# Kernel for a hybrid attention, retention and mixture-of-experts layer: the last experts' rows summed in the banks

## The reference: what is computed

```python
# g_sel: best of 4 groups; expert_id: the 2 best of its 8 experts; 32 experts in all
hid = jax.nn.silu(xb @ w_gate[e]) * (xb @ w_up[e])      # 2048 -> 512
y   = (hid @ w_down[e]) * row_w                          # 512 -> 2048
out = segment_sum(y, row_tok)                            # back to the tokens
x   = layer_norm(alpha * x + out, ln2_scale, ln2_bias)
```

## Time and profile before

| what | us |
|---|---|
| runs, median (lowest to highest) | 2056.97 (2056.35 to 2057.52) |
| the profiled execution | 2061.3 |
| its span, first to last instruction | 2059.5 |
| TensorE busy in the span | 1783.2 |
| VectorE, ScalarE busy | 995.0, 751.4 |

### The profile page before, as it was taken

How to read it: one execution, slowest core, us unless ns; L and a number is a source line. 1 busy time by engine, 2 the same in 40 slices (tenths; PEclk the granted TensorE clock), 3 DMA queues, 4 the chain that set the end, 5 groups by cost and what they waited for, 6 DMA issues and landing times.

```text
span 2059.5 us, 25116 instructions
## 1 busy us (share of the span) xinstructions
PE 1783.2 (87%) x9868; PEld 1151.2 (56%) x9868; DVE 995.0 (48%) x1469; ACT 751.4 (36%) x1321; POOL 15.3 (1%) x34
## 2 busy tenths in 40 slices
PE   9999999999999999999999977766776676666677
PEld 7888888888888888888888532211221122112222
DVE  5454454555444444566565555344433443344357
ACT  5444444344444444454453423122222222122221
POOL 0000000000000000000000000000000000000000
PEclk9999999999999999999999978777787777777778
DMA  7556655455556555466677999999999999999998
GB/s 246 193 176 191 197 176 178 148 184 188 190 184 192 171 186 176 154 191 234 221 278 290 378 430 421 429 433 432 431 433 431 432 432 430 433 431 433 431 427 335
DMA packets 131010, 615.07 MB, mean 299 GB/s; under 512 B 13108, under 2 KB 13780, under 8 KB 116720
## 3 DMA queue, kind: packets, MB, share of 16 engines
q1 hardware_dynamic: 130208, 611.74, 77.0%
q0 software_dynamic: 720, 2.18, 0.6%
HBM read 609.61 MB, written 2.36 MB: 297 GB/s over the span
## 4 chain that ended last, share of the span: by engine, by line
PE 60%; DMA 26%; issue 10%; DVE 2%; ACT 1%; DVEq 0%; POOL 0%; POOLq 0%; SPq 0%; ACTq 0%
DMA W<-in_w_expert_up_dram 25%; PE PS L603 14%; PE PS L605 14%; PE PS L604 14%; PE PS L1217 11%; PE PS L1194 2%; PE PS L1150 1%; PE PS L983 1%; PE PS L1259 1%; DVE ZACC L2267 1%; PE PS L1330 0%; DMA VC<-VS 0%; PE PS L1073 0%; PE PS L960 0%; DMA XN<-in_x_dram 0%
## 5 line engine op out<-in xcount | busy, mean ns | idle before, releaser
L580 DVE TENSOR_TENSOR WL<-RAW,WH 128x1024 fp32r<-128x1024 f32 x384 | 457.5, 1222 | 400.4 <-ACT WH L576 399.1
L576 ACT ACTIVATE WH<-RAW 128x1024 fp32r<-128x1024 f32 x384 | 394.6, 1058 | 260.8 <-PE PS L605 198.9
L603 PE MATMUL PS<-WH,XH 128*128 128x512 f32 x1216 | 479.9, 395 | 0.1
L605 PE MATMUL PS<-WH,XL 128*128 128x512 f32 x1216 | 474.0, 390 | 0.0
L604 PE MATMUL PS<-WL,XH 128*128 128x512 f32 x1216 | 473.2, 389 | 0.0
L1217 PE MATMUL PS<-W,XE 128*32 128x512 f32 x1728 | 244.8, 730 | 120.2 <-DMA W<-in_w_expert_up_dram 120.2
L603 PEld LDWEIGHTS PS<-WH,XH 128*128 128x128 f32 x1216 | 228.3, 188 | 49.5 <-issue 1.7
L605 PEld LDWEIGHTS PS<-WH,XL 128*128 128x128 f32 x1216 | 228.2, 188 | 48.6
L604 PEld LDWEIGHTS PS<-WL,XH 128*128 128x128 f32 x1216 | 228.5, 188 | 45.4
L1217 PEld LDWEIGHTS PS<-W,XE 128*32 128x32 f32 x1728 | 62.4, 131 | 321.9 <-issue 210.3
L2218 DVE TENSOR_TENSOR GSUM_H<-PS,GB 32x512 f32<-32x512 f32 x31 | 21.0, 678 | 363.0 <-ACT UB L1671 363.0
(11 more groups left out here) (335 smaller groups left out, 1530.8 us busy)
## 6 DMA issues: line engine op xcount, KB each, us to landing
RAW<-in_w_in_dram SPq DMA_DIRECT2D x304, 512.0 KB, 4.5
W<-in_w_expert_down_dram SPq DMA_DIRECT2D x28, 4096.0 KB, 29.0
W<-in_w_expert_gate_dram SPq DMA_DIRECT2D x27, 4096.0 KB, 34.8
W<-in_w_expert_up_dram SPq DMA_DIRECT2D x27, 4096.0 KB, 19.9
RAW<-in_w_branch_ret_dram SPq DMA_DIRECT2D x32, 512.0 KB, 5.1
RAW<-in_w_out_dram SPq DMA_DIRECT2D x32, 512.0 KB, 5.8
W<-in_w_expert_down_dram SPq DMA_DIRECT2D x7, 2048.0 KB, 28.1
W<-in_w_expert_gate_dram SPq DMA_DIRECT2D x7, 2048.0 KB, 10.9
```

The costliest lines, as they stand in the source:

```text
L576: act.activation(WH[:, i % RING], RAW[:, i % RING], ACT.Copy).then_inc(hi_done, 1)
L580: dve.tensor_tensor(WL[:, i % RING], RAW[:, i % RING], WH[:, i % RING].bitcast(F32), ALU.subtract).then_inc(lo_done, 1)
L603: pe.matmul(PS[:, bank + t], hs, wh, start=first and j == 0, stop=False)
L605: mm = pe.matmul(PS[:, bank + t], ls, wh, start=False, stop=end)
```

## The change

Four things at the end of the expert pipeline:

- On VectorE the weights and tokens of 30 come ahead of `add_rows(28, 0)`, and the gating of 30 and `add_rows(28, 1)` ahead of the tables. On ScalarE the tanh of 30 comes after the first half of `rows_scaled(31)`.
- The down products of 30 go to XE_BANK, from a hidden buffer of its own (HT30), right behind those of 29, whose parts get buffers of their own (YH29, YL29).
- The rows of 29 and 30 are summed in the SPREAD banks (`spread_29`, `spread_30`, `spread_both`), and VectorE adds each bank pair once (`add_both`) instead of twice.
- `spread_norm2` 2 and 3 come ahead of the second half of the last `gate_up`, and on VectorE all of `norm_rows` ahead of `hidden_last`. Two matmuls of `keep_busy` remain there where three were.

```diff
+                    if bank == XE_BANK:
+                        pe.wait_ge(xe_stored, NE * QS)
+                    elif not first:
                         pe.wait_ge(y_dve, item)
...
+        def spread_part(t, m, gs, y, start, stop):
...
+            rows = slice(m * ROWS, (m + 1) * ROWS)
+            return pe.matmul(PS[:, SPREAD + m], gs[rows, t * P:(t + 1) * P], y[rows, :], start=start, stop=stop)
...
+        def spread_29():
...
+            pe.wait_ge(g_ready, NE - 2)
+            pe.wait_ge(added, (NE - 3) * 4 + 2)
+            pe.wait_ge(y_dve, NE - 2)
+            for y in (YH29, YL29):
+                for m in range(QD):
+                    spread_part(0, m, GS29, y, y is YH29, False)
+        def spread_30():
...
+            for m in range(QD):
+                spread_part(0, m, GS30, YH, False, False)
+            pe.wait_ge(y_dve, NE - 1)
+            for m in range(QD):
+                mm = spread_part(0, m, GS30, YL, False, True)
+                if m % 2:
+                    mm.then_inc(spread, 2)
+        def spread_both(n):
+            pe.wait_ge(added, (NE - 3) * 4 + 4 + 2 * n)
+            for gs, y in ((GS29, YH29), (GS29, YL29), (GS30, YH), (GS30, YL)):
+                for m in range(2 * n, 2 * n + 2):
+                    mm = spread_part(1, m, gs, y, y is YH29, y is YL)
+            mm.then_inc(spread, 2)
...
         spread_rows(NE - 4, 1)
+        turn_hidden(NE - 2)
         down(NE - 3, 1, (2, 3), halves=True)
-        pe.wait_ge(h_ready, NE - 1)
-        turn_hidden(NE - 2)
-        spread_rows(NE - 3, 0, GS29, by_pairs=True)
-        down(NE - 2, 2, (0, 1), halves=True)
-        spread_rows(NE - 3, 1, GS29, by_pairs=True)
-        down(NE - 2, 2, (2, 3), halves=True)
-        pe.wait_ge(xe_stored, NE * QS)
-        keep_busy(XE_BANK, 1, rid, Z[:, 0, 0:CH])
-        for t in range(TOK):
-            spread_rows(NE - 2, t, GS30, by_pairs=True)
-            if t == 0:
-                keep_busy(XE_BANK, 2, rid, Z[:, 0, 0:CH])
+        down(NE - 2, 2, range(KH), halves=True, ht=HT30, bank=XE_BANK)
+        spread_29()
+        keep_busy(GU_BANK, 1, rid, Z[:, 0, 0:CH])
+        spread_30()
+        keep_busy(GU_BANK, 1, rid, Z[:, 0, 0:CH])
+        for n in range(2):
+            spread_both(n)
         number_slots()
         spread_compact(0)
-        spread_norm2(0)
+        for j in range(2):
+            spread_norm2(j)
         gate_up(NE - 1, 3, 0, take(1), last=True)
-        spread_norm2(1)
         spread_compact(1)
         gather_sums()
+        for j in range(2, 4):
+            spread_norm2(j)
         gate_up(NE - 1, 3, 1, take(1), last=True)
-        spread_norm2(3)
...
+        rows_scaled(NE - 1, 1, range(1))
         hidden_tanh(NE - 2)
-        rows_scaled(NE - 1, 1)
-        y_high(NE - 3, W29)
-        hidden_copy(NE - 2)
-        y_high(NE - 2, W30)
+        rows_scaled(NE - 1, 1, range(1, QS))
+        hidden_copy(NE - 2, HT30)
...
+        hidden(NE - 2)
+        add_rows(NE - 4, 1)
         for t in range(TOK):
             last = dve.tensor_scalar(TOKV[:, t:t + 1], RC[:, R_P:R_P + 1], float(QD),
...
-        hidden(NE - 2)
-        add_rows(NE - 4, 1)
-        y_low(NE - 3, W29)
+        y_low(NE - 3, W29, high=YH29, low=YL29)
+        y_low(NE - 2, W30, bank=XE_BANK)
         for t in range(TOK):
-            add_rows(NE - 3, t)
-        y_low(NE - 2, W30)
-        for t in range(TOK):
-            add_rows(NE - 2, t)
+            add_both(t)
         row_stats()
...
-        for j in range(2):
+        for j in range(4):
             norm_rows(j, 0)
-        centre_rows(2, 0)
         hidden_last()
-        scale_rows(2, 0)
-        norm_rows(3, 0)
```

More of the change, by code:

```diff
@@ L469, in build @@
     RSTD3 = at("RSTD3", 198.47, [1])
+    YH29 = at("YH29", 44, [QC], F32R)
+    YL29 = at("YL29", 46, [QC], F32R)
+    HT30 = at("HT30", 30.5, [KH, ROWS])
     OB = at("OB", 112, [TOK, D])
@@ L1238, in turn_hidden_more, with down @@
             mm.then_inc(h_turned, 1)
-        def down(item, k4, blocks, first=False, halves=False, more=False):
+        def down(item, k4, blocks, first=False, halves=False, more=False, ht=HT, bank=Y_BANK):
             pair_q = MORE_PAIRS[2] if more else LAST_PLACES[2, item] if halves else place(2, k4) % PAIRS
@@ L1258, in down @@
                     col = (b % KB2) * D + m * QC
-                    mm = pe.matmul(PS[m * ROWS:(m + 1) * ROWS, Y_BANK], HT[:, b],
+                    mm = pe.matmul(PS[m * ROWS:(m + 1) * ROWS, bank], ht[:, b],
                                    W[pair_q][:, b // KB2, col:col + QC], start=b == 0, stop=b == KH - 1)
@@ L1320, in spread_rows @@
                 pe.wait_ge(y_act, item + 1)
-            if not by_pairs:
-                pe.wait_ge(added, item * 4 + 2 * t + 2)
+            pe.wait_ge(added, item * 4 + 2 * t + 2)
             for part, y in ((0, YH), (1, YL)):
@@ L1326, in spread_rows @@
                 for m in range(QD):
-                    if by_pairs and part == 0 and m % 2 == 0:
-                        pe.wait_ge(added, item * 4 + 2 * t + 1 + m // 2)
                     rows = slice(m * ROWS, (m + 1) * ROWS)
-                    mm = pe.matmul(PS[:, SPREAD + m], gs[rows, t * P:(t + 1) * P], y[rows, :],
+                    mm = pe.matmul(PS[:, SPREAD + m], GS[rows, t * P:(t + 1) * P], y[rows, :],
                                    start=part == 0, stop=part == 1)
@@ L1357, in spread_norm2 @@
                 pe.wait_ge(ln2_low, 1)
-            if j < 2:
-                pe.wait_ge(added, (NE - 1 + run) * 4 + 1 + j)
+            if j < 2 and run:
+                pe.wait_ge(added, NE * 4 + 1 + j)
+            elif j < 2:
+                pe.wait_ge(added, (NE - 1) * 4 + 2 * j)
             if j >= 2:
@@ L1679, in rows_copy, with rows_scaled @@
             act.activation(xg(item)[:], PS[:, xe_bank(item)], ACT.Copy).then_inc(xg_stored, 1)
-        def rows_scaled(item, buf):
+        def rows_scaled(item, buf, parts=range(QS)):
             first = isinstance(item, int) and item < 2
             act.wait_ge(xe_turned, item + 1)
-            for j in range(QS):
+            for j in parts:
                 for k in range(KQ):
@@ L2267, in add_rows, with add_both @@
                 dve.tensor_tensor(z, PS[:, SPREAD + 2 * n:SPREAD + 2 * n + 2], z, ALU.add).then_inc(added, 1)
+        def add_both(t):
+            for n in range(2):
+                dve.wait_ge(spread, (NE - 3) * 4 + 4 * t + 2 * n + 2)
+                z = ZACC[:, t, n * 2 * QC:(n + 1) * 2 * QC].rearrange("p (m c) -> p m c", m=2)
+                dve.tensor_tensor(z, PS[:, SPREAD + 2 * n:SPREAD + 2 * n + 2], z, ALU.add).then_inc(added, 2)
         def row_stats():
```

27 lines of the change are left out of this document (17 added, 10 removed).

## The result

The changed kernel takes 2063.79 us (median of 11 runs, 2061.01 to 2065.91) beside 2058.37 for the one before (11 runs, 2056.35 to 2060.11). The ratio is 1.0027 with an interval of [1.0019, 1.0035]: slower by 5.4 us, and beyond the top of the range of the prediction (2062.0). The three runs that the prediction started from had put the kernel before at 2056.97, 1.4 lower than the eleven do.

What follows compares the result with a forecast made beforehand. Bound: the second store and LZ ending together, LZ hanging on the gating of 31. Between +0.2 (full clock) and +2.4 (half clock) it took +2.0: 2063.3 for the profile, 2059.0 for the median, range 2055.7 to 2062.0.

Steps and rivals of the forecast that it cites:

- Gating of 30: VectorE and ScalarE: HB of 30 ready at 2006.8 instead of 2010.29, 3.5 us earlier.
- Down products of 30: TensorE: wait for weights until 2012.1 and 2017.0, end at 2020.4; of the 3.5 us, 0.4 are left.
- Rows summed in the banks: From the products of 30 to the last add: 7.1 instead of 7.5, four adds back to back.
- TensorE behind the adds: Gate and up of 31 start at 2028.5 to 2029.2 behind the second spread_norm2; last half at 2039.7 to 2040.0.
- The lower clock on the last half: Last 32 gate and up matmuls, nearer the slow row: +2.4 at half clock, +0.2 at full; +2.0 taken.
- A sum of +2.0: Whole kernel: loss in us taken between +0.2 and +2.4, the last gate and up partly at full clock.
- The gating behind all norms: VectorE: gating of 31 not before 2044.4, 0.25 later than before; at the slow price 2046.7, 2.5 later.
- The second store: End of kernel: issued 7 us earlier, lands long before LZ, worth 0.1.
- The end: Last 32 down products of 31: 3.64 in the sum, with no cost for the idleness in front of them.
- a rival, with 0.20: Last 32 down products at the lower clock take 6.4 instead of 3.64: +2.7 more, 2061.7 to 2062.0; chance 0.20.

Runs made afterwards that it cites:

- the repairs: Changed kernel with VectorE's old order at the end and four fills (LAST_FILL = 4) ahead of the turning of 31, together: 2062.77, ratio 1.0015 to the kernel before.

## Why the prediction was wrong

- **Gating of 30: right.** HB was done at 2004.42. In this execution the gate and up products of 30 were 2.27 early, so 2006.8 becomes about 2004.5. Nothing behind it became late.
- **Down products of 30: right.** They waited for their weights twice, the second time until 2016.34, took 3.40 and ended at 2019.74. With the landing 0.7 later that is the 2020.4 I took. The weights set the end of this piece, so the early gating brought no more.
- **Rows summed in the banks: wrong by a little.** The prediction gave 7.1 from the products to the last add, with four adds back to back. It was 7.45. The fill (2020.34, 1.13) holds the rows of 30 up until 2021.39, though YH is there earlier, and 0.23 lies between the adds (2024.83). The 0.4 that I gave to the sums is gone: half the adds, and no gain. VectorE still waits for rows ahead of both adds (0.95 and 0.23). The Trainium skill ("Trainium Kernel Development and Optimization", Best Practices) says only that tiling doesn't speed up the evacuation of the banks; that each add taken away is then saved was my reading, and 7.47 against 7.45 doesn't bear it out.
- **TensorE behind the adds: wrong path.** The prediction had the first spread_norm2 done beside the last add and only the second behind it, so that gate and up "start at 2028.5 to 2029.2", 1.0 to 1.7 behind the adds at 2027.5. The first one began at 2027.07, with the adds nearly done (2027.19), and both stood on the path at the lower clock's price, 1.71 each (4 x 0.43; at 1.00 four took 1.03, from 2039.68 to 2040.71). The half started at 2030.61, 3.42 behind the adds. I had the earlier trace rows say that the half runs at the lower clock, and did not ask what that makes of the matmuls in front of it.
- **The lower clock on the last half: wrong place.** "the last 32 gate and up matmuls in over 5 us with PEclk near 0.5" was the sign that I named, and a 3.8 there was to prove me wrong. The second half took 3.64 at a clock of 1.00, and 3.64 in every profile in which it stands whole. What I took for idleness, a wait for the second block, was not there in the changed kernel: TensorE came so late that VectorE waited 2.49 for it. Where the wait was there, 1.09 in the new order alone, the half behind it took 3.64 too.
- **These two errors cancelled, and that is luck.** A sum of +2.0 with adds 0.8 earlier has the products end near 2045.6, about 18 behind the adds. They ended at 2045.36, 18.17 behind: the last half started at 2041.72, 1.7 to 2.0 late, as the first half before it had, and was some 2 shorter than the sum had it.
- **The gating behind all norms: the mechanism was right, the size was off.** The norms ended at 2046.59, not 2044.4, because they waited for the late spread_norm2. The gating lost 0.49 behind GB (2046.02), where the prediction gave 0.25, and only for products that end early; at +2.0 its sum had the products last and nothing for this.
- **The second store: right in kind.** It was issued at 2046.6, 4.8 earlier than before where I had 7, and had landed when LZ was done.
- **The end: the step that failed.** The sum kept the last 32 down products at 3.64 and put the idleness in front of them at nothing; it stood only as a rival, with 0.20, an idle 1.5 and last products of 6.4. The idle was 2.15 and the products took 5.13 at 0.52 and 0.62, 1.49 more. With the 0.46 that the gating lost more than before (0.49 less 0.03) this is the 1.95 by which the last piece is longer. Filled, that end took 3.64 (LAST_FILL = 4); left empty in the old order it took 5.25, and the runs lost 1.8. The rule of the Trainium skill ("TensorE: Matmul & The Clock Gate", Part 1) that the clock is low unless activity releases it fits the end, with 0.52 behind the idle stretch. It doesn't account for 2026 to 2030, where the profile has TensorE busy 2.00 of 2.00 and the clock at 0.55 and 0.50.

So the sum gave the profile +2.0 and it came to +4.08: -1.12 up to the adds (I had -0.8), +3.00 to the products (about +2.9), +1.95 to LZ (nothing), and 0.25 behind. The median missed by 4.8. Of this 2.1 is what the profile shows, nearly all of it that end, 1.4 is the base of three runs, and 1.3 is that the medians differ by 5.42 and the two profiled executions by 4.08; no run says where that part lies.

Shown by runs: the order behind the adds is the loss (1.0031 alone, 1.0005 without it); an empty end costs 1.8 (1.001 in the old order). Less sure: VectorE's order is a third to a half of the loss (0.0014 between the ratios, 0.0008 with the end filled, intervals that overlap). Read from profiles only: that fills ahead of the first half were paid at the lower clock, and how the loss divides between the two pieces. Open: what lowers the clock where the adds end, why it falls at another point in other executions, and whether the repairs add. A stretch of 4.2 us behind LZ is 5.1 to 5.7 in four of the profiles; there the last write, of LZ, takes 3.6 to 4.1 from issue to landing, and 2.7 in all others. All four have the whole new order on TensorE, but so have the changed kernel and the one with the end filled, which show 2.7; whether the order brings this about is open too, and it may hold a part of the 1.3. No version was clearly faster than the kernel before.

## What to carry to other kernels

Where the profile shows that a stretch of TensorE runs at the lower clock, price every instruction that you add inside it at that clock too. Before an operation that does off-path work is moved ahead of the critical one, ask what it filled where it stood: here the spread_norm2 behind the last products kept TensorE occupied, and without it the idle in front of the turning was 2.15 instead of 0.58. Taking away half of an engine's work gains nothing while it waits for its input: here VectorE still waited for rows ahead of both double adds.

## What the runs showed that I had not expected

- TensorE can be busy without a break and yet be granted 0.50: in 2026 to 2030 after, with 4-row matmuls, and in 2026 to 2034 of the kernel with fills among them, full matmuls included.
- The same idleness, 1.70 us, was followed by 3.64 in one execution, by 5.08 and 5.34 in two others; 0.59 or less was followed by 3.64 in all seven profiles that have it, and 2.15 or more by 4.97 to 5.25 in three.
- A new order can move the stretch at the lower clock without removing it: with the half put first it took 3.64 in one profile, and the sums behind the small matmuls went from 1.92 to 3.42; in two others the half put first took 5.55 and 6.59.
